# Three seven-product chunks in eighteen instead of ten of the 22 blocks of an up projection, and three smaller moves of waits

## What is computed

```python
def conv_ffn(h, w_up, conv_w, conv_b, w_down):      # w_up 2048 x 11264, w_down 5632 x 2048
    u = h @ w_up
    u = causal depthwise convolution of width 3 over u, + conv_b
    gate, val = jnp.split(u, 2, axis=-1)
    return (jax.nn.silu(gate) * val) @ w_down
```

## Time and profile before

| what | value |
|---|---|
| three timed runs | 2515.15, 2515.76, 2516.18 us; median 2515.76 us |
| profiled execution | 2516.16 us, its span on the core 2514.4 us |
| PE busy | 2502.3 us of the span |
| DVE busy | 2086.3 us |
| ACT busy | 1413.1 us |
| DMA | 472.29 MB, 188 GB/s over the span |

### The profile page before, as it was taken

One profiled execution on the slowest core, in us unless ns is written; L12 is line 12 of the kernel. 1 busy time (PEld: TensorE's weight loads), 2 busy tenths in 40 slices (PEclk: granted clock), 3 DMA queues, 4 the chain that ended last, 5 costly groups with the idle time before them and its releaser, 6 DMA issues.

```text
span 2514.4 us, 30571 instructions
## 1 busy us (share of the span) xinstructions
PE 2502.3 (100%) x11859; PEld 2094.3 (83%) x11859; DVE 2086.3 (83%) x2337; ACT 1413.1 (56%) x1527; POOL 28.9 (1%) x36
## 2 busy tenths in 40 slices
PE   9999999999999999999999999999999999999999
PEld 8888888888888888887888888888888888888887
DVE  6656666999999998988777878776699999999897
ACT  6545555655666655556545545544566565656554
POOL 1000000000000000000000000000000000000000
PEclk9999999999999999999999999999999999999999
DMA  8544554646465556566556666654464655556654
GB/s 281 184 159 158 190 187 145 223 159 228 166 214 183 194 195 218 192 208 193 152 158 186 186 201 186 182 170 151 141 229 167 228 174 179 206 171 228 213 166 160
DMA packets 362228, 472.29 MB, mean 188 GB/s; under 512 B 18997, under 2 KB 215813, under 8 KB 361968
## 3 DMA queue, kind: packets, MB, share of 16 engines
q1 hardware_dynamic: 360448, 465.64, 56.7%
q0 software_dynamic: 1408, 4.76, 0.6%
q10 hardware_dynamic: 240, 0.10, 0.0%
HBM read 468.31 MB, written 3.68 MB: 188 GB/s over the span
## 4 chain that ended last, share of the span: by engine, by line
PE 89%; DVE 5%; ACT 3%; DMA 2%; issue 1%; SPq 0%; ACTq 0%; DVEq 0%
PE psum L1906 38%; PE psum L1910 19%; PE psum L1792 8%; PE psum L1793 8%; PE psum L1799 8%; PE psum L2002 1%; DVE w_lo L1077 1%; DMA w_raw<-in_b_w_qkv 1%; ACT w_hi L631 1%; PE psum L1917 1%; PE psum L1919 1%; PE psum L1918 1%; PE psum L2127 1%; ACT w_hi L642 1%; DMA w_raw<-in_f_w_up 1%
## 5 line engine op out<-in xcount | busy, mean ns | idle before, releaser
L1906 PE MATMUL psum<-w_hi,xT 128*128 128x512 f32 x4056 | 993.6, 391 | 0.9
L1906 PEld LDWEIGHTS psum<-w_hi,xT 128*128 128x128 f32 x4056 | 758.2, 188 | 161.6 <-DVE xT L1449 5.1
L631 ACT ACTIVATE w_hi<-w_raw 128x2048 fp32r<-128x2048 f32 (+1 forms) x338 | 615.3, 1822 | 432.9 <-PE psum L1910 322.7
L1077 DVE TENSOR_TENSOR w_lo<-w_raw,w_hi 128x2048 fp32r<-128x2048 f32 (+1 forms) x338 | 725.6, 2167 | 86.5 <-ACT w_hi L631 86.2
L1910 PE MATMUL psum<-w_lo,xT 128*128 128x512 f32 x2028 | 527.7, 389 | 0.1
L1910 PEld LDWEIGHTS psum<-w_lo,xT 128*128 128x128 f32 x2028 | 380.5, 188 | 79.9 <-DVE w_lo L1077 1.0
L1792 PE MATMUL psum<-w_hi,xT 128*128 128x512 f32 (+1 forms) x1008 | 362.7, 369 | 2.2 <-DVE phase L1574 2.1
L1793 PE MATMUL psum<-w_hi,xT 128*128 128x512 f32 (+1 forms) x1008 | 356.0, 363 | 0.0
L1085 DVE TENSOR_TENSOR w_lo<-w_raw,w_hi 128x2048 fp32r<-128x2048 f32 (+1 forms) x118 | 255.9, 2180 | 56.8 <-ACT w_hi L642 56.5
L642 ACT ACTIVATE w_hi<-w_raw 128x2048 fp32r<-128x2048 f32 (+1 forms) x118 | 215.3, 1830 | 107.0 <-PE psum L1910 59.3
L1069 DVE TENSOR_TENSOR w_lo<-w_raw,w_hi 128x2048 fp32r<-128x2048 f32 (+1 forms) x98 | 188.7, 1941 | 59.4 <-ACT w_hi L620 59.0
(11 more groups left out here) (199 smaller groups left out, 1869.6 us busy)
## 6 DMA issues: line engine op xcount, KB each, us to landing
w_raw<-in_f_w_up SPq DMA_DIRECT2D x352, 512.0 KB, 4.9
w_raw<-in_f_w_down SPq DMA_DIRECT2D x176, 512.0 KB, 4.9
w_raw<-in_b_w_qkv SPq DMA_DIRECT2D x192, 256.0 KB, 3.9
w_raw<-in_a_w_qkv SPq DMA_DIRECT2D x94, 512.0 KB, 4.5
w_raw<-in_b_w_qkv SPq DMA_DIRECT2D x256, 128.0 KB, 2.7
w_raw<-in_a_w_o SPq DMA_DIRECT2D x16, 1024.0 KB, 5.0
w_raw<-in_b_w_qkv SPq DMA_DIRECT2D x32, 512.0 KB, 6.2
w_raw<-in_b_w_o SPq DMA_DIRECT2D x16, 1024.0 KB, 5.7
```

The costliest lines, as they stand in the source:

```text
L631: nc.scalar.activation(w_hi[:, slot, cols], w_raw[:, slot, cols], ACT.Copy).then_inc(hi_ready, 1)
L1077: nc.vector.tensor_tensor(w_lo[:, slot, cols], w_raw[:, slot, cols], w_hi[:, slot, cols], ALU.subtract).then_inc(lo_ready, 1)
L1906: pe.matmul(o, x[:, h, P * m:P * (m + 1)], hi, start=start and h == 0, stop=False)
```

## The change

Four edits. `UP_ENTRIES` gives the list `THREE` to all blocks but the first and the last of a layer, so the blocks t = 2, 4, 6 and 8 of each layer change from `TWO` to `THREE`. The constants' loads on POOL wait for the third chunk of weights (`w_in[2]`) in place of the last quarter of x. In B, the first entry of a head waits for a new semaphore `b_p6_out`, which the first of `b_combine`'s four operations raises, and the wait for `b_combined` moves to the fifth entry. In `fast_one` the product that writes the other banks comes third instead of first, and in B the wait for `b_pT_act` stands right ahead of it.

```diff
-UP_ENTRIES = [THREE if t % 2 else TWO for t in range(FB // 4)]
+UP_ENTRIES = [THREE if 0 < t < FB // 4 - 1 else TWO for t in range(FB // 4)]
...
-            pool.wait_ge(x_in[3], 16)
+            pool.wait_ge(w_in[2], landed(A0 + 2))
...
-                chain.step(nc.vector.tensor_tensor(u[:, 1, :], p6, u[:, 0, :], ALU.add))
-                chain.settle()
+                nc.vector.tensor_tensor(u[:, 1, :], p6, u[:, 0, :], ALU.add).then_inc(b_p6_out, 1)
+                dve.wait_ge(b_p6_out, h + 1)
...
-            def fast_one(c, x, mix, own, other, start, stop, high_made, low_made):
+            def fast_one(c, x, mix, own, other, start, stop, high_made, low_made, first_free=None):
 
                 high_made()
-                high(x[0], 0, c, 1, psum[:, other, :], start)
                 high(x[1], 0, c, 2, psum[:, own, :])
                 high(mix[3], 0, c, 3, psum[:, own + 2, :])
+                if first_free is not None:
+                    first_free()
+                high(x[0], 0, c, 1, psum[:, other, :], start)
                 low_made()
...
+                    def first_free():
+                        at_least(pe, b_pT_act, h)
...
                     if e == 0:
+                        at_least(pe, b_p6_out, h)
+                    if e == 4:
                         at_least(pe, b_combined, h)
...
-                    if e == B_ONES[0] and not is_turn(h, 0):
-                        pe.wait_ge(b_pT_act, h)
```

More of the change, by code:

```diff
@@ L382, in trunk @@
         down_quarter = sem("down_quarter")
-        b_p1_out, b_combined, b_summed = sem("b_p1_out"), sem("b_combined"), sem("b_summed")
+        b_p1_out, b_p6_out, b_combined, b_summed = sem("b_p1_out"), sem("b_p6_out"), sem("b_combined"), sem("b_summed")
         h_mixed, h_mix_hi, h_mix_lo = sem("h_mixed"), sem("h_mix_hi"), sem("h_mix_lo")
@@ L2149, in b_entry_of @@
                 else:
+                    def first_free():
+                        at_least(pe, b_pT_act, h)
                     i = MIXED.index(j)
                     mix = [mixT[:, s, i, :, :] for s in range(4)]
-                    (fast_one if what == "one" else fast_sum)(c, x, mix, own, other, i == 0, i == len(MIXED) - 1,
-                                                              high_made, low_made)
+                    begun, ended = i == 0, i == len(MIXED) - 1
+                    if what == "one":
+                        fast_one(c, x, mix, own, other, begun, ended, high_made, low_made, first_free if begun else None)
+                    else:
+                        fast_sum(c, x, mix, own, other, begun, ended, high_made, low_made)
             def upper_first(c, x, own, h):
```

## The result

| kernel | median of the timed runs | ratio to the kernel before, 95% interval |
|---|---|---|
| before | 2515.79 us | |
| with the change | 2522.57 us | 1.0026 [1.0015, 1.0037] |

The change makes the kernel 6.5 us slower by the ratio, between 3.8 and 9.3 us; the medians lie 6.8 us apart. The profiled executions' spans are 2514.4 us before and 2519.9 us after, 5.5 us apart.

What follows compares the result with a forecast made beforehand. PE bounds the kernel, busy 2502.3 of 2514.4 us. 2516.16 - 5.4 (products) - 3.2 (seams) - 1.0 (start) + 15.3 (PE's waits) = 2521.9, or 2521.5 us for the timed median; 8 in 10 range 2509 to 2528 us.

Steps and rivals of the forecast that it cites:

- Products saved: Up stage: `THREE` has 183 matmuls, `TWO` 186; eight blocks changed to `THREE` save 5.4 us of PE time.
- DVE's period, 43.17 us and its wait: `THREE` behind `THREE`: DVE's 43.17 us plus 1.07 us waiting for its own load make 44.24, against PE's 43.28.
- The other idle time, 0.24 us: DVE before 549.54, waiting for an ACT split that hangs on PE's `turn_u`; goes when DVE runs later against PE.
- The mean of nine rows: DVE's wait before the next block's first split: 1.07 us, mean of all but the last of ten `THREE` blocks.
- What is late next: PE waits for `combined` behind each of blocks t = 2 to 9 in both layers, costing 15.3 us.
- The seams: B's heads: the earlier semaphore removes PE's waits for line 1574, gaining 3.2 us, bounds 0 and 3.6.
- the wait would come again at the fifth entry: Rival, B's part: seams and start give nothing because the next wait is there at once; 2525.7 us, chance 0.08.
- The start: Constants' loads start 1.5 us earlier, PE's 0.93 us wait before the transposes goes; gain 1.0 us, bounds 0 and 1.1.
- `fast_one`, nothing: Product order in `fast_one`: same matmuls, and the wait for `b_pT_act` repeats one already passed; costs nothing.
- The rival that DVE keeps pace: Up stage: the wait at 574.65 for ACT's first-chunk split fades, PE never waits; 2506.2 us, chance 0.15 for 2506 to 2511.
- The prediction's reason for the difference: First chunk's load: 5.2 us against the page's 4.4, since the page doesn't count the next chunk's load running too.

Runs made afterwards that it cites:

- the half load: Changed kernel, loading only the left half of each tile's columns for the first chunk of blocks t = 1 to 10: 2504.71 us, 0.9957 of the kernel before.
- the wait filled: Changed kernel with DVE's `combine` and ACT's p1 copy ahead of the split of the next block's first chunk in `THREE` blocks: 2508.85 us, 0.9974 of before.

## Why the prediction was right

The forecast was 2521.5 us, 5.7 us above the median of before in this comparison; measured are 2522.57 us and 6.8 us (6.5 by the ratio). The mechanism held: a wait of about 1 us that stays in DVE's period, and PE's waits for `combine` behind blocks 2 to 9.

- **Products saved, 5.4 us.** 24 matmuls fewer on the page. What they save alone shows where nothing waits: windows of 43.25 to 43.28 us with the half load for all eight blocks of a layer, where four of them were 43.93 to 43.96 before.
- **DVE's period, 43.17 us and its wait.** Held. With waits of 0.9 to 1.4 us, 1.1 in the mean, the windows are 44.0 to 44.5 us and their means 44.24 and 44.21 us in the two layers, for the forecast's 44.24. The other idle time, 0.24 us, went as said. The mean of nine rows was a choice, though: the tenth was 2.25 us, which nothing explained and which did not come back.
- **What is late next, 15.3 us.** The windows give 7.7 + 7.7 = 15.4 us, 16 waits, each for line 1140, as said. By the rows a wait is 0.6 us in the mean, not the forecast's 0.8, since a wait costs some 0.35 us more than its row says. The list of entries alone cost 8.8 us where 15.3 - 5.4 = 9.9 was forecast, within its interval.
- **The seams, 3.2 us.** 3.5 us alone (1.3 to 5.8), 2.9 us between the means of the kept traces with and without the edit. The rows it was priced from were those of the execution with the longest such waits. That the wait would come again at the fifth entry fell.
- **The start, 1.0 us.** Mis-sized: 0.3 us between the two traces and not measurable. The step assumed that only the wait ahead of the transposes stands in the way; the constants' loads now start 1.2 us earlier, ACT splits the fourth chunk at 25.76 where it was 24.59 before, and the copies of the constants are late next. That this could take the gain away was named, with 0 as the lower bound. With 0.3 us here the forecast would have been 0.7 us higher and nearer to what was measured; that is less than the noise.
- **`fast_one`, nothing.** Confirmed alone.
- **The rival that DVE keeps pace** gave 2506.2 us for a wait of nothing. It didn't happen by itself, because the trip moves with DVE, but it is what two edits brought about: 2504.7 us with the trip cut short and 2508.9 us with the wait filled. For the load, the Trainium skill, DMA: Bandwidth & Descriptors, "Anatomy of one DMA", has an estimate of 4.4 us, by a fit that it gives for transfers issued by GpSimd. It didn't hold for SP's loads here: the two trips shown are 5.2 and 5.5 us from issue to ACT's start. The prediction's reason for the difference, the next chunk's load 1.7 us behind, is not borne out. In the changed kernel's trace the 20 such loads land 5.0 to 5.5 us after their first issue, median 5.1; the median of the up stages' 45 loads that no other one overlaps by more than 0.25 us is 5.1 as well. So the longer trip was there without the sharing, and going by the row was right for another reason than the one given.

What stays open is why some loads are later than others: in the changed kernel DVE waits longest, 1.4 us, for the load that landed last, 5.5 us after its issue. Late loads also keep the version with `combine` first about 3 us above its forecast.

## What to carry to other kernels

Where an engine's queue holds a piece of work and, some pieces later, needs a transfer that this very piece releases, the time from release to use is a part of the engine's own period: falling behind doesn't shorten it, as it did the idle time of 0.24 us here. Before shifting work to an engine that is "96% busy", add up its instructions in the new order plus what is left of such trips and set that against the other engine's period, block behind block; a surplus of 1 us a block cost 15.4 us, nearly three times the 5.4 us that the saved matmuls gave. The mending is to put work that doesn't need the transfer between release and use: the order alone turned 6.5 us of loss into 6.5 us of gain. And a term of a few us that is priced from the waits of one trace needs a second one: the seams' recorded waits were 0.2 to 2.1 us from one execution to the next.

## Not expected of the hardware

A wait of PE that its row gives with 0.54 us lengthens the window by 0.90 us (44.18 against 43.28) at the end of block 3 in the changed kernel.

```profile
581.24 3.06 PE L1906 MATMUL psum<-w_hi,xT 128*128 128x512 f32 x12 [0.54 <-DVE phase L1140]
```

The overlap of matmuls' ends explains 0.16 us (a matmul's row lasts 0.39 us, and the next one starts after 0.23). The rest is a slow restart. In an unbroken stream twelve matmuls last 11 x 0.227 + 0.39 = 2.89 us and here 3.06, 0.17 us more. The first is followed by the next after 0.34 us (0.33 at B's seam before, 1191.24 to 1191.57), and the ten steps after that are 0.22 to 0.24 us, 0.233 in the mean. With 0.54 us of idle time this makes 0.87 of the 0.90 us. Why the restart is slow no run here shows; the granted clock was 1.00 throughout.
